# Clears of the modulation's sums and of the late gate's row on GpSimd, and three low halves ahead of a wait

## The chip, the core and the metric

The kernel runs on one core of a Trainium2 chip. The core has five engines that share a memory of 128 partitions: TensorE (matmuls), VectorE, ScalarE, GpSimd, and SyncE, which only issues transfers. Each engine runs its own list of instructions in order and waits on semaphores. Transfers are issued from a queue of SyncE's and one of ScalarE's, and move on the same 16 DMA engines. The metric is the device time of one execution in microseconds. In the rows, PE is TensorE, PEld its weight load, DVE VectorE, ACT ScalarE, POOL GpSimd and SP SyncE; ACTq and SPq are what those engines issue.

## The reference

A model of two blocks of two layers each, over 256 tokens of width 1024, all in fp32. The change is in the first block, where each of the four sublayers (mixer, MLP, mixer, MLP) is modulated by a vector c:

```python
def ada_modulation(c, w, b):
    m = jax.nn.silu(c) @ w + b
    shift, scale, gate = jnp.split(m[:, None, :], 3, axis=-1)
    return shift, scale, 1.0 + gate

for layer in range(DEPTH):
    shift, scale, gate = ada_modulation(c, ada_w[layer, 0], ada_b[layer, 0])
    y = mixer(x * (1.0 + scale) + shift)          # mixer_ab in layer 0, mixer_c in layer 1
    x = layer_norm(DN_ALPHA * x + gate * y, ln_g[layer, 0], ln_b[layer, 0])
    shift, scale, gate = ada_modulation(c, ada_w[layer, 1], ada_b[layer, 1])
    h = x * (1.0 + scale) + shift
    y = jnp.square(jax.nn.relu(h @ w1)) @ w2      # D_FF = 4096
    x = layer_norm(DN_ALPHA * x + gate * y, ln_g[layer, 1], ln_b[layer, 1])
```

The second block (a recurrent mixer, an attention mixer and two MLPs) has no modulation.

## The kernel before

**Weights.** All weights pass as 193 units of 128 x 2048 fp32 (1 MB) through four slots. SyncE loads a unit into `raw`, ScalarE writes its high half (`hi`, line 1279), VectorE the low half `raw - hi` (`low`, line 1859), and TensorE multiplies with both. SyncE loads unit u + 4 when the low half of u is done, so the low halves set when weights are fetched. An fp32 product is made of three products of halves.

**An MLP** (`mlp`, once for each engine) has 16 pairs of units: an up unit (T) gives 256 columns of h @ w1, ScalarE takes them from PSUM (line 1372), VectorE squares them and splits the result into `u_hi` and `u_lo` (lines 1888 to 1902), and a down unit (D) adds u @ w2 into four PSUM banks. TensorE's order is up 0, up 1, down 0, up 2, down 1, up 3, down 2 and so on. VectorE's order at the start is square 0, an affine (the layer norm's gain and bias, lines 1824 and 1825), square 1, an affine, three low halves (for down 1, up 3 and down 2), and then the loop, which begins with square 2.

**Modulations beside it.** Only the first two of the four modulations are made on TensorE. The others are sums on VectorE: `ada_acc` (3 x 1024) is cleared, the bias row `ada_b[s]` is loaded into its first partition, and for each of 8 slices of `ada_w` a multiply with a column of silu(c) is added (lines 1869 and 1945); TensorE then sums the partitions. The call `mlp(0, M0, 2, 1)` makes modulation 2 in MLP 0 (`s_ada` = 2, three parts a slice), and also the gate of modulation 1 (`s_gate` = 1), the late gate: its row `gate_r` is cleared, a bias row is loaded, and 8 slices are added (`late`, line 1882), the first two ahead of the loop. In `mlp(1, M1, None, 3)` there is only the late gate. The mixer of layer 1 makes modulation 3 (two parts); its step `("gate", 2)` stands ahead of it, where the gate of modulation 2 is read out of `ada_acc`.

**Order of the loads.** They are issued by ScalarE in its own order of work. In an MLP, after the high halves of the first units: the layer norm's rows (`load_rows`, lines 1421 and 1422), then `ada_begin` (it waits for the clear by `acc_zero`, then the bias row, line 1357, and three slices, line 1360), then the late gate (it waits for its clear by `late_zero`, bias row, line 1385, and two slices, line 1352).

**Clears.** VectorE makes all four of `ada_acc` and `gate_r` (lines 2021 and 1909): at the start of each MLP for `gate_r`, in MLP 0 after its two affines for `ada_acc`, and at the step `("gate", 2)` for modulation 3. GpSimd does little: small powers for the norms (line 1751), in the order of the same list `STEPS`.

Of the kernel before, what the change touches and what calls it, by code (L numbers as in the profile page):

```python
# [11 lines left out]
KT = D // P  # L12
# [67 lines left out]
def two_block_kernel(nc, stream, ada_w, ada_b, x, x_t, pos, cols, ln_g, ln_b, sinks, g_norm, final_norm,  # L80
# [6 lines left out]
    with ctx:  # L87
# [45 lines left out]
        def arena(at, *shape):  # L133
            n = 1
            for s in shape:
                n *= s
            v = A[:, at:at + n]
            if len(shape) == 2:
                v = v.rearrange("p (a b) -> p a b", a=shape[0])
            return v  # L140
# [7 lines left out]
        ada_acc, gate_r = arena(ADAC, 3 * D), arena(GATE, D)  # L148
# [19 lines left out]
        def adas_before(s_, k=0, part=0):  # L168

            return KT * (0, 2, 4, 7)[s_] + SUMS[s_] * k + part  # L170
# [59 lines left out]
        late_used, late_bias, late_zero = map(sem, ("late_used", "late_bias", "late_zero"))  # L230
# [265 lines left out]
        def _(sp):  # L496
# [33 lines left out]
            def swap(r):  # L530

                tmp, _, to, w = rope_to[r]
                sp.wait_ge(turn_f, r + 1)
                for at in range(0, P, 32):
                    sp.dma_start(A[at:at + 32, to:to + w], A[at ^ 32:(at ^ 32) + 32, tmp + 512 * (r % 2):][:, 0:w]).then_inc(
                        halves_of(r)[0], 16)
# [33 lines left out]
        def _(pe):  # L570
# [300 lines left out]
            def qk_pair(k):  # L871

                heads = [head(k), head(k + 1)]
                at = 4 if k % 4 == 0 else 2
                for h in heads:
                    all_of(h["units"])
                if at == 2:
                    for b in (2, 3):
                        claim(b)
                        held[b] = (exp_done, k + b - 1)  # L880
                elif k >= 4:
                    pe.wait_ge(exp_done, k - 2)
                part = lambda e, t: B[at + e][:, 0:128] if t == 0 else B[at + e][:, 128:384]
                for e in range(2):
                    for t in range(TT):
                        q, kk, _, _ = heads[e]["qk"][0]
                        pe.matmul(part(e, t), q[:, P * t:P * t + P], kk[:, 0:P * (t + 1)], start=t == 0, stop=False,  # L887
                                  skip_group_check=True)
                for t in range(TT):
                    for e in range(2):  # L890
                        q, kk, off, w = heads[e]["qk"][1]
                        pe.matmul(part(e, t), q[off:off + w, P * t:P * t + P], kk[off:off + w, 0:P * (t + 1)], start=False,
                                  stop=False, skip_group_check=True)
                for e in range(2):
                    pe.matmul(B[at + e].rearrange("p (a b) -> p a b", b=256)[:, :, 0:P], ident_b[:, :],
                              causal_b[:, :].unsqueeze(1).to_broadcast([P, 2, P]), start=False, stop=True,
                              skip_group_check=True).then_inc(s_done, 1)
# [153 lines left out]
            for step in STEPS:  # L1051
# [128 lines left out]
                elif kind in ("down", "last"):  # L1180
# [19 lines left out]
                    else:  # L1200
# [3 lines left out]
                                  among_last if n["turned"] == "lb" else None)  # L1204
                elif kind == "bound":
                    b, what, _, _, second, units = a
                    if b in RAW:
                        continue
# [532 lines left out]
        @block.gpsimd  # L1741
        def _(g):
            made = [0]
            g.memset(minus_half[:, :], -0.5).then_inc(half_set, 1)
            g.wait_ge(half_set, 1)

            def root(c0, w, done):

                made[0] += 1
                g.wait_ge(var_ready, made[0])  # L1750
                g.tensor_tensor(rstd[:, c0:c0 + w], ve[:, c0:c0 + w], minus_half[:, 0:w], ALU.pow).then_inc(done, 1)

            for step in STEPS:
                kind, a = step[0], step[1:]
                if kind == "norm2":
                    if a[1] == ML:
                        root(2, 2, root_out)
                    root(0, 2, root_out)
                elif kind == "hg_out":
                    root(8 * a[0], 8, root_out)  # L1760
                elif kind == "bound":
                    b, what = a[0], a[1]
                    if b in RAW:
                        continue
                    for t in range(TT):
                        if b < 4:
                            root(t, 1, root_out)
                        else:
                            root(t, 1, rstd_ready)
                    if what == "lnrms":  # L1770
                        root(2, 2, root_out)
# [3 lines left out]
        def _(v):  # L1775
# [80 lines left out]
            def low(u, s):  # L1856

                v.wait_ge(hi_done, u + 1)
                v.tensor_tensor(w_lo[:, s, :], raw[:, s, :], w_hi[:, s, :], ALU.subtract).then_inc(lo_done, 1)  # L1859
# [12 lines left out]
            def mlp(m, u0, s_ada, s_gate):  # L1872
                p0 = n["plain"]

                def late(k, used, i=0):

                    at = k if isinstance(i, int) else 0
                    col = silu_c[:, k:k + 1] if isinstance(i, int) else silu_c[:, bass.ds(i + k, 1)]
                    loads = 16 * (7 * m + 1) if at == 0 else 16 * (m + 1)
                    v.wait_ge(ld_late[at], loads if isinstance(i, int) else 16 * i + (loads + 16))  # L1880
                    v.wait_ge(late_used, used)
                    v.scalar_tensor_tensor(out=gate_r, in0=late_w[at], scalar=col, in1=gate_r,
                                           op0=ALU.mult, op1=ALU.add).then_inc(late_used, 1)
# [20 lines left out]
                def low_ahead(u, i=0):  # L1904

                    low(4 * i + (u + SLOTS), u % SLOTS)

                if s_gate:
                    v.memset(gate_r, 0.0).then_inc(late_zero, 1)
                for k in range(2):  # L1910
                    square(k, k, n["step"], None)
                    n["step"] += 1
# [1 line left out]
                        normalised()  # L1914
                        affine(k)
                st = n["step"] - 4
                if s_ada:
                    zero_acc()
                    v.wait_ge(ld_bias, 16 * (s_ada + 1))
                for u in range(u0, u0 + 3):  # L1920
                    low_ahead(u)
                if s_gate:
                    v.wait_ge(late_bias, 16 * (m + 1))
                    for k in range(2):
                        late(k, KT * m + k)
# [91 lines left out]
                            f[:, c], e[:, c], lb_c[:, 1, m:m + 1], lb_c[:, 0, m:m + 1], ALU.mult, ALU.add))  # L2017
                    v.tensor_scalar(k, f, -1.0, 1.0, ALU.mult, ALU.add).then_inc(silu_done, 1)

            def zero_acc():  # L2020
                v.memset(ada_acc, 0.0).then_inc(acc_zero, 1)


            v.memset(zero8[:, :], 0.0)
            v.memset(ones[:, :], 1.0).then_inc(consts_ready, 1)
# [45 lines left out]
            for step in STEPS:  # L2071
                kind, a = step[0], step[1:]
# [16 lines left out]
                    angles()  # L2089
                elif kind == "rest":  # L2090
                    low(a[0], a[0] % SLOTS)
                elif kind in ("gate", "gate0"):
                    if kind == "gate":
                        v.wait_ge(gate_ps, a[0] + 1)
                        zero_acc()
                elif kind == "fill":
                    u, part, parts, form, src, reader, dst = a
                    n["plain"] += reader in ("plain", "value")
# [121 lines left out]
                elif kind == "duo":  # L2220
                    g, first, last = a
# [34 lines left out]
                elif kind == "bound":  # L2256
# [227 lines left out]
                    for u in (last_unit + SLOTS - 1, last_unit + SLOTS):  # L2484
                        low(u, u % SLOTS)
                elif kind == "mlp":
                    mlp(a[0], a[1], a[2], a[3])
                elif kind == "hg_start":
                    v.wait_ge(ld_level, 16)
# [54 lines left out]
                elif kind == "hg_out":  # L2544
# [3 lines left out]
                    gate = arena(H_G, TT, D)[:, t, :].rearrange("p (h v) -> p h v", h=HG_HEADS)  # L2548
# [117 lines left out]
```

## Time and profile before

| | |
|---|---|
| median of 3 runs | 1414.03 us (1412.78 to 1414.73) |
| the profiled execution | 1415.55 us, of which the span is 1413.7 |
| TensorE, VectorE, ScalarE, GpSimd busy | 1324.4, 1009.4, 594.2, 13.1 us |
| granted clock of TensorE, mean | 0.975 |
| transfers | 264.18 MB, mean 187 GB/s |

The span is from the first to the last instruction of the profiled execution; times in the rows count from its start. In a timeline a row is: start, duration from the first to the last of the row's instructions, engine, line, operation, tiles, count, and in brackets the idle time before it with what ended it. A granted clock of 1.00 is 2.4 GHz, 0.50 is 1.2 GHz.

### The profile page before, as it was taken

To read this page: it belongs to the slowest core of one execution; us is meant where nothing else is said; L and a number is where in the kernel's file an instruction comes from. 1 tells how busy PE (TensorE), PEld (TensorE's weight loads), DVE (VectorE), ACT (ScalarE), POOL (GpSimd) and SP (SyncE) were. 2 spreads that over 40 slices of the span, in tenths; PEclk is the share of its full clock that TensorE was granted. 3 is DMA by queue.
4 is the path that set the end of the run, shared out by engine and by line. 5 is a ranking of instruction groups with operands and counts; after the bars stand their busy time and mean duration, and the time that the engine had idled before them with its cause. 6 is when DMAs were issued, how large, how long until landed. Compare 5 with 4: busy or idle time off the path is not lost.

```text
span 1413.7 us, 20736 instructions
## 1 busy us (share of the span) xinstructions
PE 1324.4 (94%) x7932; PEld 1119.8 (79%) x7932; DVE 1009.4 (71%) x1358; ACT 594.2 (42%) x803; POOL 13.1 (1%) x22
## 2 busy tenths in 40 slices
PE   5897989999998989999999989999999998999997
PEld 1763677888797868888889987888888877888886
DVE  1768498888888878867687884766668665666665
ACT  2534443433344544343354322534337553533432
POOL 0000000000000000000000000000000000000000
PEclk7899999999999999999999999999999999999999
DMA  9656329878367536665535330555553331455540
GB/s 382 261 194 220 119 90 360 312 262 304 128 244 260 161 120 238 243 226 199 200 129 208 129 120 9 206 202 190 196 178 134 110 145 35 171 219 189 203 150 30
DMA packets 45791, 264.18 MB, mean 187 GB/s; under 512 B 5399, under 2 KB 7063, under 8 KB 19994
## 3 DMA queue, kind: packets, MB, share of 16 engines
q1 hardware_dynamic: 32624, 218.19, 42.2%
q10 hardware_dynamic: 13102, 45.09, 9.2%
q8 instruction: 46, 0.75, 0.2%
q14 instruction: 19, 0.16, 0.0%
HBM read 260.89 MB, written 1.05 MB: 185 GB/s over the span
## 4 chain that ended last, share of the span: by engine, by line
PE 79%; DVE 12%; ACT 3%; DMA 3%; issue 2%; SPq 0%; POOL 0%; ACTq 0%; DVEq 0%; POOLq 0%
PE banks L587 16%; PE banks L589 15%; PE banks L588 15%; PE banks L937 14%; PE banks L940 7%; DMA A<-ada_w 3%; DVE w_lo L1859 2%; PE banks L1237 2%; PE banks L817 1%; PE banks L764 1%; PE banks L799 1%; PE banks L887 1%; ACT w_hi L1279 1%; PE banks L1105 1%; DVE mx L1970 1%
## 5 line engine op out<-in xcount | busy, mean ns | idle before, releaser
L1859 DVE TENSOR_TENSOR w_lo<-raw,w_hi 128x2048 fp32r<-128x2048 f32 x193 | 439.5, 2286 | 118.7 <-ACT w_hi L1279 116.1
L1279 ACT ACTIVATE w_hi<-raw 128x2048 fp32r<-128x2048 f32 x193 | 368.4, 1914 | 226.6 <-PE banks L589 205.1
L937 PE MATMUL banks<-hT,w_hi 128*128 128x512 f32 x896 | 280.8, 395 | 0.0
L587 PE MATMUL banks<-w_hi,R 128*128 128x512 f32 (+1 forms) x624 | 245.7, 394 | 7.1 <-DVE R L1839 3.7
L589 PE MATMUL banks<-w_hi,R 128*128 128x512 f32 (+1 forms) x624 | 242.7, 389 | 0.0
L588 PE MATMUL banks<-w_lo,R 128*128 128x512 f32 (+1 forms) x624 | 242.6, 389 | 0.0
L940 PEld LDWEIGHTS banks<-hT,w_lo 128*128 128x128 f32 x896 | 168.3, 188 | 39.2
L940 PE MATMUL banks<-hT,w_lo 128*128 128x256 f32 x896 | 176.0, 278 | 0.0
L587 PE MATMUL banks<-hT,w_hi 128*128 128x256 f32 x536 | 158.3, 295 | 7.5 <-DVE hT L2329 5.6
L588 PE MATMUL banks<-hT,w_hi 128*128 128x256 f32 x536 | 153.6, 286 | 0.0
L589 PE MATMUL banks<-hT,w_lo 128*128 128x256 f32 x536 | 153.4, 286 | 0.0
L937 PEld LDWEIGHTS banks<-hT,w_hi 128*128 128x128 f32 x896 | 140.6, 189 | 4.4
L587 PEld LDWEIGHTS banks<-w_hi,R 128*128 128x128 f32 x624 | 118.0, 189 | 30.8 <-issue 7.3
L589 PEld LDWEIGHTS banks<-w_hi,R 128*128 128x128 f32 x624 | 117.9, 189 | 24.6
L588 PEld LDWEIGHTS banks<-w_lo,R 128*128 128x128 f32 x624 | 118.1, 189 | 22.0 <-issue 0.7
L1372 ACT ACTIVATE A<-banks 128x512 f32<-128x512 f32 x56 | 33.5, 598 | 216.8 <-PE banks L940 204.1
L587 PEld LDWEIGHTS banks<-hT,w_hi 128*128 128x128 f32 x536 | 104.9, 196 | 12.3 <-ACT A L1295 4.6
L587 PE MATMUL banks<-w_hi,hT 128*128 128x256 f32 (+1 forms) x320 | 103.2, 322 | 10.6 <-DVE hT L1839 8.7
L588 PEld LDWEIGHTS banks<-hT,w_hi 128*128 128x128 f32 x536 | 104.9, 196 | 1.6 <-issue 1.4
L589 PEld LDWEIGHTS banks<-hT,w_lo 128*128 128x128 f32 x536 | 104.7, 195 | 0.0
L589 PE MATMUL banks<-w_hi,hT 128*128 128x256 f32 (+1 forms) x320 | 101.0, 316 | 0.0
L588 PE MATMUL banks<-w_lo,hT 128*128 128x256 f32 (+1 forms) x320 | 100.9, 315 | 0.0
(266 smaller groups left out, 1495.3 us busy)
## 6 DMA issues: line engine op xcount, KB each, us to landing
raw<-stream SPq DMA_DIRECT2D x193, 1024.0 KB, 4.9
A<-ada_w ACTq DMA_DIRECT2D x73, 512.0 KB, 5.6
A<-ada_w SPq DMA_DIRECT2D x5, 1024.0 KB, 17.0
raw<-ada_w SPq DMA_DIRECT2D x3, 1024.0 KB, 7.5
X<-ada_w SPq DMA_DIRECT2D x2, 1024.0 KB, 4.9
A<-ln_g ACTq DMA_DIRECT2D x4, 512.0 KB, 3.6
A<-ln_b ACTq DMA_DIRECT2D x4, 512.0 KB, 5.6
A<-ada_w SPq DMA_DIRECT2D x1, 1536.0 KB
```

The costliest lines, as they stand in the source:

```text
L587: pe.matmul(o, lh, rh, start=start, stop=False, skip_group_check=True)
L588: pe.matmul(o, lh, rl, start=False, stop=False, skip_group_check=True)
L589: return pe.matmul(o, ll, rh, start=False, stop=stop, skip_group_check=True)
L764: m = pe.transpose(B[b][:, P * i:P * i + P], tile, ident[:, :])
L799: pe.matmul(B[d["bank"] + e][:, P * t:P * t + P * (t + 1)], d["q"][r, P * t:P * t + P], d["k"][r, 0:P * (t + 1)], start=t == 0, stop=False ...
L817: m = pe.matmul(B[6 + e][:, P * i:P * i + P], d["p"][e][:, P * i:P * i + P], d["diag"][e][:, 0:P] if i == 0 else d["diag"][e][:, P:2 * P], ...
L937: pe.matmul(two(B[2 * kp + a]), wh[:, kt, P * a:P * a + P], hT[:, :, kt, :], start=kt == 0, stop=False, skip_group_check=True)
L940: last = pe.matmul(B[2 * kp + a][:, 0:256], wl[:, kt, P * a:P * a + P], hT_hi[:, kt, :], start=False, stop=kt == KT - 1, skip_group_check= ...
L1237: m = pe.matmul(bank[:, P * (i % 4):P * (i % 4) + P], tile_at(H_K, h)[:, P * t:P * t + P], tile_at(H_Q, h)[:, P * tq:P * tq + P], start=Tr ...
L1279: act.activation(w_hi[:, s, :], raw[:, s, :], ACT.Copy).then_inc(hi_done, 1)
L1372: act.activation(two(u_f[:, kp, :]), banks[:, 2 * kp:2 * kp + 2, 256:512], ACT.Copy).then_inc(fill_read, 1)
L1859: v.tensor_tensor(w_lo[:, s, :], raw[:, s, :], w_hi[:, s, :], ALU.subtract).then_inc(lo_done, 1)
```

## The change

GpSimd takes the four clears, each behind a wait of its own. It clears `ada_acc` for modulation 2 at the step `row_out`, when TensorE has used the last slice of modulation 1 (`row_w` and the row before it lie in the same place); for modulation 3 at the step `gate`, when the gate has been summed into PSUM (`gate_ps`); and `gate_r` at the step `mlp`, when the residual of the mixer ahead has read the gate (`y_read`). The semaphores `acc_zero` and `late_zero` that ScalarE waits for stay. In an MLP with sums, VectorE's three low halves stand in front of its wait for the bias row (`ld_bias`) instead of behind it.

```diff
--- before.py
+++ after.py
@@ gpsimd, in the loop over STEPS
+                elif kind == "row_out":
+                    g.wait_ge(ada_used, adas_before(1, KT))
+                    g.memset(ada_acc, 0.0).then_inc(acc_zero, 1)
+                elif kind == "gate":
+                    g.wait_ge(gate_ps, a[0] + 1)
+                    g.memset(ada_acc, 0.0).then_inc(acc_zero, 1)
+                elif kind == "mlp" and a[3]:
+                    m = a[0]
+                    g.wait_ge(y_read, 4 * (2 * m + 1))
+                    g.memset(gate_r, 0.0).then_inc(late_zero, 1)
@@ vector, mlp
-                if s_gate:
-                    v.memset(gate_r, 0.0).then_inc(late_zero, 1)
                 for k in range(2):
                     square(k, k, n["step"], None)
...
-                if s_ada:
-                    zero_acc()
-                    v.wait_ge(ld_bias, 16 * (s_ada + 1))
                 for u in range(u0, u0 + 3):
                     low_ahead(u)
+                if s_ada:
+                    v.wait_ge(ld_bias, 16 * (s_ada + 1))
                 if s_gate:
                     v.wait_ge(late_bias, 16 * (m + 1))
@@ vector
-            def zero_acc():
-                v.memset(ada_acc, 0.0).then_inc(acc_zero, 1)
...
-                elif kind in ("gate", "gate0"):
-                    if kind == "gate":
-                        v.wait_ge(gate_ps, a[0] + 1)
-                        zero_acc()
```

## Rows read from the trace of the kernel before

**Rows 1.** The page's part 4, the chain that ended last, by engine.
```profile
PE 79%; DVE 12%; ACT 3%; DMA 3%; issue 2%; SPq 0%; POOL 0%; ACTq 0%; DVEq 0%; POOLq 0%
```

**Rows 2.** Timeline of VectorE at the start of MLP 0 (start us, us, ...).
```profile
200.91 0.91 DVE L1909 MEMSET A<- 128x1024 f32 x1 [0.16 <-issue]
...
210.96 2.62 DVE L2021 MEMSET A<- 128x3072 f32 x1 [0.71 <-DVE X L1825]
215.96 6.69 DVE L1859 TENSOR_TENSOR w_lo<-raw,w_hi 128x2048 fp32r<-128x2048 f32 x3 [2.38 <-DMA A<-ada_b]
...
224.66 1.28 DVE L1882 SCALAR_TENSOR_TENSOR A<-A,silu_c 128x1024 f32<-128x1024 f32 x1 [0.82 <-DMA A<-ada_w]
```

**Rows 3.** Timeline of TensorE in MLP 0: starts of its second and third down stages.
```profile
218.38 0.49 PE L587 MATMUL banks<-w_hi,R 128*128 128x512 f32 x1 [2.16 <-DVE w_lo L1859]
...
231.11 0.40 PE L587 MATMUL banks<-w_hi,R 128*128 128x512 f32 x1
```

**Rows 4.** One stretch of the windows: us, busy times, PEclk, DMA share, GB/s.
```profile
219.00:220.00 1.00, 1.00 (x4) 0.81 (x3) 1.00 (x1) 0.16 (x1) 0.00 (x0) 0.50 1.00 410
```

**Rows 5.** Timeline of ScalarE's queue in MLP 0.
```profile
211.14 0.46 ACTq L1422 DMA_DIRECT2D A<-ln_b  x1
213.61 0.25 ACTq L1357 DMA_DIRECT2D A<-ada_b  x1
...
215.58 0.91 ACTq L1352 DMA_DIRECT2D A<-ada_w  x2
```

**Rows 6.** Timelines of VectorE, ScalarE's queue and TensorE in MLP 1.
```profile
549.93 6.70 DVE L1859 TENSOR_TENSOR w_lo<-raw,w_hi 128x2048 fp32r<-128x2048 f32 x3
...
562.63 1.28 DVE L1882 SCALAR_TENSOR_TENSOR A<-A,silu_c 128x1024 f32<-128x1024 f32 x1 [2.40 <-DMA A<-ada_w]
...
565.82 0.69 DVE L1902 TENSOR_TENSOR R<-A,R 128x512 fp32r<-128x512 f32 x1
...
550.84 0.46 ACTq L1422 DMA_DIRECT2D A<-ln_b  x1
...
566.77 0.40 PE L587 MATMUL banks<-w_hi,R 128*128 128x512 f32 x1
```

**Rows 7.** Timelines of VectorE, ScalarE, its queue and TensorE in layer 1's mixer.
```profile
401.84 2.62 DVE L2021 MEMSET A<- 128x3072 f32 x1 [0.59 <-issue]
...
399.72 1.26 ACT L1434 ACTIVATE A<-banks,ones 128x512 f32<-128x512 f32 x2 [7.37 <-PE banks L1046]
...
403.63 1.93 ACT L1279 ACTIVATE w_hi<-raw 128x2048 fp32r<-128x2048 f32 x1
404.49 0.26 ACTq L1357 DMA_DIRECT2D A<-ada_b  x1
...
437.60 1.65 PE L799 MATMUL banks<-A 64*128 64x128 f32 x8 [4.33 <-DVE A L2147]
```

**Rows 8.** DMA queues (packets, MB, share): 210.8-216, 210.8-226, then 558-560 twice; q10 ScalarE's.
```profile
q10 hardware_dynamic: 334, 1.24, 71.0%
...
q10 hardware_dynamic: 1012, 3.69, 64.7%
...
q1 hardware_dynamic: 75, 0.57, 67.7%
q10 hardware_dynamic: 75, 0.28, 34.5%
```

**Rows 9.** Timelines: the last slice's matmuls, VectorE behind them, a power on GpSimd.
```profile
149.28 1.06 PE L1005 MATMUL banks<-A,silu_c 128*32 128x512 f32 x8
...
151.76 0.48 DVE L1987 TENSOR_SCALAR A<-ident,ri 128x128 f32<-128x128 f32 x2
...
187.71 0.55 DVE L2308 TENSOR_SCALAR A<-X,mv,rstd 128x512 f32<-128x512 f32 x1
...
859.16 1.74 POOL L1751 TENSOR_TENSOR rstd<-ve,minus_half 128x8 f32<-128x8 f32 x1 [4.99 <-DVE ve L2554]
...
860.05 0.42 DVE L1838 CAST R<-A 128x512 fp32r<-128x512 f32 x1
```

## The prediction

> **What bounds the kernel now.** I read the page first: its chain of work is 79% TensorE, 12% VectorE and 3% DMA [rows 1]. So VectorE work that goes away is worth only the TensorE stalls that it causes, and I looked for stalls beside the four clears that the change takes from VectorE.
>
> MLP 0 (the timelines of 196 to 235 us, then the windows): VectorE, when its second affine is done, clears the sums at 210.96 for 2.62, then idles 2.38 for the bias row and begins its three low halves only at 215.96 [rows 2]. TensorE's first down matmul that needs the first of them starts at 218.38 after 2.16 of idling [rows 3], and after that stall its granted clock is 0.50, the lower level of 1.2 GHz [rows 4]. ScalarE's queue explains the wait: the layer norm's rows go out at 211.14, and the bias row only at 213.61, when the clear has ended; the two late gate slices go out from 215.58 [rows 5].
>
> MLP 1 is the useful neighbour. It has the same layer norm rows and late gate, but no sums, so there the three lows already follow the affine with nothing between. The queue's second row load goes out at 550.84 against 211.14: MLP 1 is MLP 0 shifted by 339.70. Its third down stage starts at 566.77 with no stall; its u is complete at 565.82 + 0.69 = 566.51, so it had 0.26 us to spare, and what ran last before it was the second late gate slice, whose multiply had waited until 562.63 for its data [rows 6].
>
> The mixer of layer 1: VectorE clears from 401.84 for 2.62, ScalarE's bias load goes at 404.49, and TensorE later idles 4.33 for the roped keys, on a chain of ada_w loads begun there [rows 7]. The four clears of the two MLPs and the mixer are all that is in question; elsewhere the kernel stays as it is.
>
> **Part 1, what goes from VectorE.** Two clears of 2.62, two of 0.91 and one wait of 2.38 [rows 2, 7]. The late row's 0.91 in MLP 0 stands ahead of the first square, but the second square waits for ScalarE all the same, so I count 0 to 0.9 and take nothing; in MLP 1 TensorE does not stall, and it is worth 0.
>
> **Part 2, MLP 0 up to the first down stage.** The bias load no longer waits for a clear. ScalarE's queue goes on after its second row load (211.14 and its 0.46), so everything behind it goes out some 2.0 earlier: bias at 211.6, three ada_w slices to 213.2, the late bias and the two late slices by 214.4. VectorE starts the lows at 549.93 - 339.70 = 210.2, 5.7 earlier. The stall of 2.16 goes. Undisturbed, TensorE would start its third down stage at 566.77 - 339.70 = 227.07; it started at 231.11 [rows 3, 6], so stall and low clock together cost 4.04, of which the clock is about 1.7 (4.04 less the stall, which measured from the modelled end before it may be 2.3). If nothing is late next, this part gives -4.0.
>
> **What is late next.** The lows free their raw slots, so SyncE's three 1 MB weight loads also go out 5.9 earlier, at about 212.5, 214.7 and 217.0, as in MLP 1. In the kernel before, they went out behind the ada_w and late slices: from 210.8 to 216 ScalarE's queue alone moved bytes (1.24 MB), and its 3.69 MB were through by 226 [rows 8]. Now they compete, with 3.69 - 1.24 = 2.45 MB still to come on ScalarE's queue at 216, and the late slices are the last of it. In MLP 1, where they do compete, SyncE's queue moved 0.57 MB and ScalarE's 0.28 in the same 2 us: twice as much, 0.425 MB/us together [rows 8]. MLP 1 has only 0.26 to spare with 1.5 MB fewer in that queue, so MLP 0 must now wait. When does the second late slice land?
> - Upper bound: all of both queues must pass first, 2.45 + 3.15 = 5.60 MB, 13.2 us, 229.2. At 2 to 1 it comes out there too, since the weights are through first.
> - Equal shares: 2 x 2.45 / 0.425 = 11.5 us, 227.5.
> - Lower bound, strictly in order of issue with one weight load ahead: 3.50 / 0.425 = 8.2 us, 224.2.
>
> I take 228.5, near the 2 to 1 of the row. From the late multiply to a complete u is 566.51 - 562.63 = 3.88 [rows 6]. So the third down stage starts at 232.4 in place of 231.11: +1.3. TensorE has then idled 5.3 from 227.07, and the low clock after it costs 1.7 as it did after 2.16: MLP 0 is **+3.0** and not -4.0. Bounds: 224.2 gives 228.1 and -3.0 (with a full clock cost -1.3); 229.2 and half a microsecond to land gives +4.2. Behind that stage VectorE is in time again (low, three sums of 1.28 like the late multiply's, low, square: its next u about 2 us ahead of need), so the shift is passed on unchanged.
>
> **Part 3, the mixer.** GpSimd can start its clear when the gate rows are in PSUM, the moment at which ScalarE reads them (399.72), and at VectorE's 2.62 it ends at 402.3. ScalarE comes to its bias load when its second high half has started, 403.63, instead of 404.49. So the ada_w chain, up to the stall at 437.60, begins 0.8 earlier [rows 7]: **-0.8**. If GpSimd needs twice VectorE's time the clear ends at 405.0 and this becomes +0.5; if every load still lands when it did, 0.
>
> **Part 4, the clears on GpSimd.** No row shows a long clear on GpSimd. Three of the four have much room: the sums' first from about 150.3 (the last ada_w slice's matmuls, 149.28 and 1.06) to 211.6, the late rows 25 us. What they can cost is VectorE's own time beside them. From below: a GpSimd power of 1.74 us at 859.16 ran while VectorE's cast at 860.05 took 0.42, its usual time, so 0 [rows 9]. From above: the diagonal multiplies at 151.76 would wait for the clear's end at 150.34 + 2.62 = 152.96, 1.2, on the chain there; the centred half at 187.71 for a clear of 0.91 begun at about 187.3, 0.5 [rows 2, 9]: 1.7 together. The power touched only 8 columns, so the row is weak evidence; I take **+0.4**.
> The Trainium skill ("SBUF — State Buffer", "Who interferes with whom") says that casts and scalar multiplies of VectorE which stream through two ports share them with GpSimd under an exclusive lock, and the loser waits for the whole instruction; two-input operations don't mind a GpSimd that only writes. The cast at 860.05 does not show it; by the rule the sum would have the upper 1.7 here.
>
> **Sum.** +3.0 - 0.8 + 0.4 = +2.6 us. The profiled execution took 1415.55, with a span of 1413.7 and 1.85 around it, and is 1.5 above the median of the runs, 1414.03; the shift holds for both, so I put 1414.03 + 2.6 = **1416.6**. A difference under 0.2% (2.8 us) is about what a measurement of this kernel can't tell from none.
>
> **Rivals.**
> - *Nothing is late next* (the other side): the late slices land before 223.2 and MLP 0 gives its 4.0, the mixer 0.8: 1409.2. For it: the second landed by 224.66 before [rows 2], issued 2 us later. Against: then the weight loads were behind them. It decides at a landing of 223.2 (227.07 - 3.88). Chance 0.10.
> - *The queues share in the late slices' favour*: landing between 224.2 and 226.5, start of the stage 228.1 to 230.4, low clock 0 to 1.7; with the mixer and the clears -3.4 to +0.6: 1410.6 to 1414.6. For it: the slices are issued first, and in MLP 1 the two shares were measured with no ada_w slices queued. Against: 2 to 1 is what MLP 1 shows. Chance 0.20.
> - *A clear on GpSimd holds up VectorE* at 151.76 and 187.71 for its whole length: 1.3 more than in the sum, +3.9: 1417.9. Decided by a cast or scalar multiply that starts within a clear. Chance 0.20. The rule of the Trainium skill ("SBUF — State Buffer", "Who interferes with whom") would make it so.
> - *The change doesn't free ScalarE*: a GpSimd clear slower than 3.9 us (403.63 - 399.72) holds the mixer's bias load; at 8 us (three times VectorE's) it goes out at 407.7, 3.2 later than before, which is 4.0 more than in the sum: 1420.6. Chance 0.08.
> - *The forecast*, weight loads first and little on VectorE: +1.3 to +3.7, 1415.3 to 1417.7. Chance 0.42.
>
> Faster by over 0.2%: the first rival and half of the second's lower part, 0.18. Slower: about 0.4 of the forecast's 0.42 (0.17), the third rival (0.19) and the fourth (0.07), 0.43. Within 0.2%: the rest, 0.39. The range of 8 in 10, 1411.2 to 1419.2, leaves out the first rival, the edge of the second and the fourth; the forecast's own is 1415.3 to 1417.7.
>
> **What would show it.** In MLP 0: low halves right behind the affine (about 210.2), no stall at the first of the loop's down stages, the late multiplies waiting some 10 us for ada_w, and a TensorE stall of about 5 us some 11 us after the old one, named after the u, with a granted clock of 0.5 behind it. In the mixer: the bias load 0.8 earlier against the gate rows. At the diagonal multiplies after the last ada_w slice: no gap, or one as long as the clear. It would be wrong if the late multiplies started within 13 us of the affine's end, or if the mixer's stall were shorter by much more than 0.8.

## Result and the profile after

The changed kernel takes 1423.62 us (median of 10 runs), the kernel before 1415.36 in the same session (10 runs): a ratio of 1.0055, 95% interval 1.0038 to 1.0071, which is 7.8 us slower (5.4 to 10.0). The forecast was 1416.6, that is +2.6, with a range up to 1419.2: the sign of its sum is right, its size is not. (1.3 of the distance is the kernel before itself, whose first three runs had a median of 1414.03.) The profiled execution of the changed kernel took 1427.3 with a span of 1425.4; it is 3.7 above the median of its ten runs, so I compare it stage by stage and not by its end. The ratios of the experiments leave out four executions of 2196 to 4804 us (one each of e4 and e5, two of the kernel before), which the medians still count.

The chain of work that ended last now has DMA in it at 4%, which had 3% [rows 1]:

```profile
PE 80%; DVE 10%; DMA 4%; ACT 3%; issue 2%; SPq 0%; ACTq 0%; POOL 0%; DVEq 0%; POOLq 0%
```

**MLP 0.** The timeline of VectorE, against [rows 2]; the three low halves now begin where the affine (from 213.99 for 1.22) ends:

```profile
215.25 6.69 DVE L1869 TENSOR_TENSOR w_lo<-raw,w_hi 128x2048 fp32r<-128x2048 f32 x3
234.71 2.69 DVE L1892 SCALAR_TENSOR_TENSOR A<-A,silu_c 128x1024 f32<-128x1024 f32 x2 [12.77 <-DMA A<-ada_w]
239.31 0.69 DVE L1912 TENSOR_TENSOR R<-A,R 128x512 fp32r<-128x512 f32 x1
```

TensorE, against [rows 3], and the windows, against [rows 4]. The stall of 2.16 at the second down stage is gone; in its place stands one of 7.81 at the third, and the clock behind it is the lower level again (0.50, the third figure from the end of a row of the windows):

```profile
240.05 0.80 PE L587 MATMUL banks<-w_hi,R 128*128 128x512 f32 x1 [7.81 <-DVE R L1912]
248.40 0.61 PE L937 MATMUL banks<-hT,w_hi 128*128 128x512 f32 x2
```
```profile
241.00:242.00 1.00, 1.00 (x4) 0.73 (x3) 1.00 (x1) 0.00 (x0) 0.00 (x0) 0.50 0.06 16
244.00:245.00 1.00, 1.00 (x4) 0.74 (x3) 1.00 (x2) 0.00 (x0) 0.00 (x0) 0.50 0.90 352
```

ScalarE's queue, against [rows 5], the weight loads on SyncE's, and the queues' bytes (packets, MB, share) in three stretches of 2 us, 219 to 221, 225 to 227 and 233 to 235:

```profile
215.79 0.34 ACTq L1421 DMA_DIRECT2D A<-ln_g  x1
216.65 0.30 ACTq L1357 DMA_DIRECT2D A<-ada_b  x1
218.93 1.01 ACTq L1352 DMA_DIRECT2D A<-ada_w  x2
```
```profile
217.71 4.74 SPq L498 DMA_DIRECT2D raw<-stream  x3
```
```profile
q10 hardware_dynamic: 134, 0.51, 62.7%
...
q1 hardware_dynamic: 84, 0.56, 66.1%
q10 hardware_dynamic: 82, 0.29, 35.1%
...
q10 hardware_dynamic: 154, 0.53, 65.6%
q1 hardware_dynamic: 23, 0.07, 8.4%
```

The row 225 to 227 is the 2 to 1 that [rows 8] showed in MLP 1, now with ada_w slices queued. It holds until the weights are through at 233; then ScalarE's queue is alone again, and the late slices are the last of it.

**The diagonal multiplies and the centred half**, against [rows 9]: GpSimd's clears in its timeline, then VectorE's multiplies in its own. The first pair took 0.48 before and ends here at 155.86, the clear at 155.72; the half took 0.55:

```profile
153.06 2.66 POOL L1763 MEMSET A<- 128x3072 f32 x1 [107.31 <-PE banks L1005]
190.84 0.94 POOL L1770 MEMSET A<- 128x1024 f32 x1
413.20 2.66 POOL L1766 MEMSET A<- 128x3072 f32 x1 [14.94 <-PE banks L1046]
```
```profile
154.36 1.50 DVE L1994 TENSOR_SCALAR A<-ident,ri 128x128 f32<-128x128 f32 x2
...
191.32 0.75 DVE L2308 TENSOR_SCALAR A<-X,mv,rstd 128x512 f32<-128x512 f32 x1
```

**The mixer of layer 1**, against [rows 7]: ScalarE and its queue, then TensorE at the scores. The third clear ends at 415.86, and the bias row goes out at once, while the first high half is still running and 1.19 before the second:

```profile
413.18 1.27 ACT L1434 ACTIVATE A<-banks,ones 128x512 f32<-128x512 f32 x2 [7.29 <-PE banks L1046]
...
414.81 1.92 ACT L1279 ACTIVATE w_hi<-raw 128x2048 fp32r<-128x2048 f32 x1
415.90 0.26 ACTq L1357 DMA_DIRECT2D A<-ada_b  x1
...
417.09 1.93 ACT L1279 ACTIVATE w_hi<-raw 128x2048 fp32r<-128x2048 f32 x1
```
```profile
448.47 0.93 PE L799 MATMUL banks<-A 64*128 64x128 f32 x8 [2.73 <-DVE A L2147]
```

**Stages.** To compare executions I use differences of starts. "MLP 0" is from the issue of its first layer norm row (215.79 above, 210.78 before) to GpSimd's power in the next norm:

```profile
386.73 0.54 POOL L1751 TENSOR_TENSOR rstd<-ve,minus_half 128x1 f32<-128x1 f32 x1 [194.95 <-DVE ve L1809]
```
In the kernel before, with the start of the up stage that follows its third down stage, which is needed below:
```profile
210.78 0.34 ACTq L1421 DMA_DIRECT2D A<-ln_g  x1
...
236.56 0.62 PE L937 MATMUL banks<-hT,w_hi 128*128 128x512 f32 x2
...
374.90 0.54 POOL L1751 TENSOR_TENSOR rstd<-ve,minus_half 128x1 f32<-128x1 f32 x1 [187.63 <-DVE ve L1799]
```

386.73 - 215.79 = 170.94 against 374.90 - 210.78 = 164.12. "Diagonals" is from one low half to the next around the diagonal multiplies (before: 149.37 and 167.15). "Mixer" is from ScalarE's reading of the gate rows to the power of the mixer's own norm (before: 399.72 and 519.01). The kernels e1 to e12 are those of the next section.

| execution | MLP 0 | diagonals | mixer |
|---|---|---|---|
| before / once more (e10) | 164.12 / 163.81 | 17.78 / 17.78 | 119.29 / 118.71 |
| after / once more (e11) | 170.94 / 170.71 | 18.79 / 18.82 | 115.24 / 115.39 |
| e1 clears alone | 164.49 | 18.79 | 115.71 |
| e2 order alone | 168.55 | 17.78 | 117.16 |
| e3 late slices first | 160.08 | 21.29 | 114.23 |
| e4 quiet clears | 170.50 | 17.79 | 115.70 |
| e5 mixer's clear alone | 163.79 | 17.81 | 115.91 |
| e6 late first and quiet | 160.08 | 17.83 | 115.74 |
| e7 weight loads split | 168.18 | 18.80 | 117.27 |
| e8 clear in pieces | 170.21 | 18.08 | 114.25 |
| e9 bias row ahead | 170.65 | 18.82 | 115.23 |
| e12 late first, VectorE's clears | 160.08 | 17.78 | 118.80 |

The 21.29 of e3 has a low clock in it (0.83 over 150 to 165, where the kernel before has 1.00).

Between the second of these low halves (167.15 before, 170.76 after) and the first layer norm row lies a stretch that the table leaves out. It takes 43.63 and 43.60 in the two executions of the kernel before and 45.03 and 44.80 in those of the changed kernel. The centred half stands in it, and a stretch of low clock behind it, which ends later in the changed kernel; the windows, 29 us behind the low half in each, after and then before:

```profile
200.00:201.00 1.00, 1.00 (x6) 1.00 (x6) 1.00 (x2) 0.00 (x0) 0.00 (x0) 0.50 0.00 0
...
196.00:198.00 2.00, 2.00 (x19) 2.00 (x18) 2.00 (x2) 0.00 (x0) 0.00 (x0) 1.00 0.45 61
```

MLP 1, which the prediction put at 0, shows no gain: from the last power ahead of it to the next it takes 185.96 and 186.83 before, 186.86 and 186.88 after.

### The profile page after: what moved, and what is told of

The parts are those of the page before. It is cut to its first block, busy times and chain, and to the rows that moved or that the text cites. A ratio compares the mean times of both kernels' runs of the same rounds, so it can differ in the third digit from the quotient of the medians.

```text
span 1425.4 us, 20737 instructions
## 1 busy us (share of the span) xinstructions
PE 1331.4 (93%) x7932; PEld 1125.5 (79%) x7932; DVE 1004.3 (70%) x1354; ACT 594.4 (42%) x803; POOL 20.2 (1%) x26
## 4 chain that ended last, share of the span: by engine, by line
PE 80%; DVE 10%; DMA 4%; ACT 3%; issue 2%; SPq 0%; ACTq 0%; POOL 0%; DVEq 0%; POOLq 0%
PE banks L587 16%; PE banks L588 16%; PE banks L589 16%; PE banks L937 14%; PE banks L940 7%; DMA A<-ada_w 4%; PE banks L1237 2%; DVE w_lo L1869 2%; PE banks L817 1%; PE banks L764 1%; PE banks L799 1%; PE banks L887 1%; PE banks L1105 1%; ACT w_hi L1279 1%; PE banks L832 1%
```

## Experiments

**e1 and e2: one half of the change each.** e1 keeps the clears on GpSimd and restores the order; e2 has only the order.

```diff
 e1, against after                            e2, against before
+    if s_ada: v.wait_ge(ld_bias, ...)        +    for u in range(u0, u0 + 3): low_ahead(u)
     for u in range(u0, u0 + 3): low_ahead(u)      if s_ada: v.wait_ge(ld_bias, ...)
-    if s_ada: v.wait_ge(ld_bias, ...)        -    for u in range(u0, u0 + 3): low_ahead(u)
```

> The changed kernel with VectorE's wait for the bias row back in front of the three low halves of MLP 0; the clears stay on GpSimd. Theory (the early lows send SyncE's weight loads out among the late gate slices, and these get a third of the bytes): the lows begin some 3.7 us later than in the changed kernel, the weight loads go out as much later, the late multiply starts some 14.5 to 16 us behind the affine's end instead of 19.5, and TensorE's stall before the third down stage falls from 7.8 to about 3 to 4: 3 to 5 us faster than the changed kernel. Rival (the clears on GpSimd, or ScalarE's queue being two microseconds early, are what costs): late multiply, stall and time as in the changed kernel.

> The kernel before with only the order changed: the three low halves in front of the wait for the bias row in MLP 0; every clear stays on VectorE. Theory (weight loads against late slices): lows begin at about 3 us behind the affine's end (the clear is still there), no stall at the first of the loop's down stages, late multiply some 17 us behind the affine's end, TensorE idles 3 to 5 us before the third down stage with the low clock behind it: MLP 0 is 1 to 4 us longer than in the kernel before; the mixer of layer 1 and the diagonal multiplies (0.48 us) as before: 1416 to 1419 us. Rival (the order itself is harmless and the clears make the loss): MLP 0 is 2 to 4 us shorter than before, 1411 to 1413.

e1: 1416.54, ratio to before 1.0012 (0.9993 to 1.0031). e2: 1421.74, ratio 1.0039 (1.0018 to 1.0059). So the order makes the loss in MLP 0: with it alone the stage is 4.4 longer, without it 0.4. The rest of the changed kernel's 6.8 needs both parts: in e2 the lows still begin 3.25 behind the affine's end, after VectorE's clear, and in the changed kernel right behind it. VectorE, TensorE and the queues (221 to 223, then 225 to 227) of e1:

```profile
218.59 6.70 DVE L1869 TENSOR_TENSOR w_lo<-raw,w_hi 128x2048 fp32r<-128x2048 f32 x3 [6.12 <-DMA A<-ada_b]
225.21 2.68 DVE L1892 SCALAR_TENSOR_TENSOR A<-A,silu_c 128x1024 f32<-128x1024 f32 x2
```
```profile
221.02 0.49 PE L587 MATMUL banks<-w_hi,R 128*128 128x512 f32 x1 [2.52 <-DVE w_lo L1869]
```
```profile
q10 hardware_dynamic: 229, 0.84, 102.1%
...
q1 hardware_dynamic: 108, 0.81, 97.3%
q10 hardware_dynamic: 4, 0.01, 1.1%
```

Here ScalarE's queue moves alone until 223, when little of its work is left, and the weights come after it. The late multiplies run straight behind the lows, with no wait at all: the expected stall of 3 to 4 us before the third down stage isn't there, and MLP 0 is 6.4 shorter than in the changed kernel's first profile, where 3 to 5 was expected. What I had not expected is the wait of 6.12: without a clear to wait for, the bias row was issued 0.86 behind the first layer norm row (2.83 in the kernel before), and the lows began 5.54 behind it (5.18 before). Nothing was gained by freeing the queue.

In e2 (TensorE):

```profile
235.49 0.80 PE L587 MATMUL banks<-w_hi,R 128*128 128x512 f32 x1 [6.03 <-DVE R L1902]
```

The stall was expected at 3 to 5, and the time at 1416 to 1419: both came out above.

**e9: the bias row ahead of the layer norm rows.** To see what e1's wait is.

```diff
 scalar, mlp (against e1)
+    if s_ada: ada_bias(s_ada)       # the row's load, out of ada_begin
     if m < 2: load_rows(m, 1)
     if s_ada: ada_begin(s_ada)      # now the three slices alone
```

> The clears alone on GpSimd, with the three lows behind the wait for the bias row as in the kernel before, but ScalarE issues that bias row ahead of the two layer norm rows. Theory (freeing ScalarE's queue gained nothing for the bias row because it lands behind the two 512 KB layer norm rows in front of it): the row lands about 2.5 us after its issue instead of 4.7, the lows begin 2 to 3.5 us earlier than with the clears alone (some 3 us behind the affine's end instead of 6.1), the weight loads follow, and the late multiply comes that much nearer to the changed kernel's 19.5 us behind the affine's end: a stall of 1 to 4 us before the third down stage. Rival (the row's own single partition is what takes 4.7 us): lows as with the clears alone.

One run, 1428.0 us. ScalarE's queue, VectorE and TensorE:

```profile
216.23 0.25 ACTq L1356 DMA_DIRECT2D A<-ada_b  x1
216.52 0.34 ACTq L1427 DMA_DIRECT2D A<-ln_g  x1
```
```profile
218.09 6.70 DVE L1875 TENSOR_TENSOR w_lo<-raw,w_hi 128x2048 fp32r<-128x2048 f32 x3 [2.44 <-DMA A<-ada_b]
...
236.55 1.28 DVE L1898 SCALAR_TENSOR_TENSOR A<-A,silu_c 128x1024 f32<-128x1024 f32 x1 [1.76 <-DMA A<-ada_w]
```
```profile
240.49 0.80 PE L587 MATMUL banks<-w_hi,R 128*128 128x512 f32 x1 [7.81 <-DVE R L1918]
```

The row is there 1.9 us after its issue (218.09 - 216.23), where it took 4.7 in e1: it had stood behind two transfers of 512 KB. And the lows, 2.4 behind the affine's end, give the whole stall of the changed kernel and not a part: by this one execution it isn't the lows' start in proportion that counts, but whether the weight loads come in while the slices still have bytes to move.

**e3, e6 and e12: the late slices first.** In e3 ScalarE issues the late bias and slices ahead of the modulation's, and VectorE waits in that order; e6 adds e4's waits (below); e12 is the same order in the kernel before with the lows ahead, all clears on VectorE.

```diff
 scalar, mlp                                   vector, mlp
-    if s_ada: ada_begin(s_ada)               -    if s_ada: v.wait_ge(ld_bias, ...)
     if s_gate: late bias, two late slices         if s_gate: wait for late_bias, late(0), late(1)
+    if s_ada: ada_begin(s_ada)               +    if s_ada: v.wait_ge(ld_bias, ...)
```

> The changed kernel, but in MLP 0 ScalarE issues the late bias and the two late gate slices ahead of the modulation's bias row and ada_w slices, and VectorE's wait for that bias row stands behind the late multiplies. Theory (the late slices are late only because they are last in a queue that gets a third of the bytes): the late multiply starts some 12.5 us behind the affine's end as in MLP 1, TensorE does not idle before the third down stage, and MLP 0 is 9 to 11 us shorter than in the changed kernel and about 4 shorter than before: 1412 to 1415 us. Rival (ScalarE's queue as a whole is late): the three ada_w slices become what TensorE waits for one stage on, and the time falls by less than 4 us.

> The changed kernel with the late gate slices issued ahead of the modulation's and with GpSimd's first clear behind the diagonal multiplies and its row clear behind the first lows of the loop. If the three findings add up: MLP 0 some 160 us from its layer norm rows to the next norm (164.1 before, 170.9 changed), diagonal multiplies 0.48, mixer 114 to 117: 5 to 8 us faster than the kernel before, 1408 to 1411. If the lock costs nothing end to end: no faster than the run with the late slices first alone (1413.6).

> The kernel before with every clear still on VectorE; the three lows stand in front of the wait for the bias row, and ScalarE issues the late slices ahead of the modulation's. Theory (in MLP 0 the order of the loads decides, and where the clears run is worth little): no stall before the third down stage, MLP 0 some 161 us from its layer norm rows, 2 to 4 us faster than the kernel before: 1412 to 1414. Rival (the clear on VectorE still delays the lows or the late slices' row enough): MLP 0 above 163 us, no faster than the kernel before.

e3: 1413.57, ratio to before 0.9978 (0.9957 to 0.9999). e6: 1411.32, 0.9967 (0.9949 to 0.9986). e12: 1414.36, 0.9978 (0.9958 to 0.9999). All three have 160.08 in MLP 0 and no stall of TensorE at its start: 10.9 less than the changed kernel and 4.04 less than before (3.73 against its second execution), as the prediction worked out for nothing being late. VectorE in e3, where the second late multiply stands 11.5 behind the affine's end (218.28):

```profile
226.25 1.28 DVE L1892 SCALAR_TENSOR_TENSOR A<-A,silu_c 128x1024 f32<-128x1024 f32 x1 [1.24 <-issue]
229.79 1.28 DVE L1892 SCALAR_TENSOR_TENSOR A<-A,silu_c 128x1024 f32<-128x1024 f32 x1 [2.26 <-DMA A<-ada_w]
```

The modulation's slices, last now, cost TensorE nothing. By e12 the stage needs none of GpSimd's clears for this. e6 has the lowest median of all kernels here, 4.7 below before where 5 to 8 was expected; e3, e6 and e12 are not told apart by their intervals.

**e7: SyncE's weight loads in halves.**

```diff
 sync, load (against after); ScalarE's wait counts 32 a unit
-    sp.dma_start(raw[:, s, :], w).then_inc(raw_full[s], 16)
+    sp.dma_start(raw[:, s, 0:1024], w[:, 0:1024]).then_inc(raw_full[s], 16)
+    sp.dma_start(raw[:, s, 1024:2048], w[:, 1024:2048]).then_inc(raw_full[s], 16)
```

> The changed kernel, but SyncE loads each 1 MB weight tile as two transfers of 1024 columns, so that a row of a weight transfer is 4 KB as in the ada_w slices, and no longer 8 KB. Theory (the engines take the queues' rows in turn, so bytes go 2 to 1 because the rows are 2 to 1): while both queues have work in MLP 0 each moves about half, and the late multiply starts some 1 to 2.5 us earlier behind the affine's end than 19.5 us. Rival (the ratio goes by the queue or by what was there first): 2 to 1 stays and the late multiply is where it was. The time may also move by what twice as many transfers cost elsewhere.

1426.86, ratio to before 1.0078 (1.0049 to 1.0107): no faster than the changed kernel in all, though MLP 0 is 2.7 shorter. Its queues at 224 to 226, VectorE and TensorE:

```profile
q10 hardware_dynamic: 115, 0.42, 51.5%
q1 hardware_dynamic: 117, 0.42, 51.1%
```
```profile
229.76 1.28 DVE L1894 SCALAR_TENSOR_TENSOR A<-A,silu_c 128x1024 f32<-128x1024 f32 x1 [9.84 <-DMA A<-ada_w]
232.14 1.28 DVE L1894 SCALAR_TENSOR_TENSOR A<-A,silu_c 128x1024 f32<-128x1024 f32 x1 [1.10 <-DMA A<-ada_w]
```
```profile
236.09 0.80 PE L589 MATMUL banks<-w_hi,R 128*128 128x512 f32 x1 [5.87 <-DVE R L1914]
```

With rows of 4 KB in both queues each moves 0.42 MB in 2 us, and the second late multiply begins 18.9 behind the affine's end instead of 20.8 (the first, of which the expectation spoke, 16.6 instead of 19.5). The packets were near one to one in the changed kernel too (84 and 82): the queues share by packets, and 2 to 1 in bytes was 8 KB against 4.

**e4 and e8: GpSimd's first clear.** e4 lets it wait for the eight diagonal multiplies, and the clear of `gate_r` for the first lows of the loop; e8 makes it in six pieces.

```diff
 gpsimd (against after), e4                    e8
+    g.wait_ge(duo_ready, 8)                   -    g.memset(ada_acc, 0.0)...
     g.memset(ada_acc, 0.0)...                 +    for c in range(0, 3 * D, 512):
...                                            +        p = g.memset(ada_acc[:, c:c + 512], 0.0)
+    g.wait_ge(lo_done, a[1] + 2)              +    p.then_inc(acc_zero, 1)
     g.memset(gate_r, 0.0)...
```

> The changed kernel, but GpSimd's first clear of the sums waits until VectorE's eight diagonal multiplies are through, and its clear of the late gate's row until the first lows of the loop are done. Theory (a clear on GpSimd holds up a scalar multiply of VectorE for its whole length): the diagonal multiply falls from 1.50 to 0.48 us, the centred half from 0.75 to 0.55, and the time by about 1.2 us. Rival (the long multiply of the one profile was something else): they keep their lengths or the time does not move by more than 0.5 us.

> The changed kernel, but GpSimd's first clear of the sums is made of six clears of 512 columns, some 0.5 us each. Theory (VectorE's scalar multiply waits for the GpSimd instruction that holds the port, and for that one alone): the diagonal multiply that took 1.50 us takes at most 1.0 (0.48 and what is left of one piece). Rival (the loser waits until GpSimd has nothing more to do): it takes 1.5 us or more, as the six pieces end no earlier than the one clear.

e4: 1419.59, ratio to before 1.0032 (1.0013 to 1.0052); the multiplies take 0.48 and the half 0.55 again, and the stretch of the diagonals is 17.79, 1.0 less than after. The 1.2 us by themselves are below what the times can tell: e4's interval overlaps that of the changed kernel. e8, one run, 1423.81; GpSimd and VectorE:

```profile
153.14 2.99 POOL L1764 MEMSET A<- 128x512 f32 x6 [107.31 <-PE banks L1005]
```
```profile
154.44 0.76 DVE L1996 TENSOR_SCALAR A<-ident,ri 128x128 f32<-128x128 f32 x2
```

The multiplies ended at 155.20 with the pieces running until 156.13: VectorE waits for the piece that is under way and not for GpSimd to be done.

**e5: the mixer's clear alone.** The kernel before with only the third clear on GpSimd.

```diff
 gpsimd                                        vector
+    elif kind == "gate":                     -    elif kind in ("gate", "gate0"):
+        g.wait_ge(gate_ps, a[0] + 1)         -        if kind == "gate":
+        g.memset(ada_acc, 0.0)...            -            v.wait_ge(...); zero_acc()
```

> The kernel before with one part of the change: GpSimd does the clear in front of the mixer of layer 1; the other three clears and the order stay. Theory (ScalarE's queue issues ahead of its activations, so the bias load goes out at the clear's end and not behind the second high half): the bias load 2.7 us after the gate rows are read instead of 4.8, the stall at the scores shorter or gone, the mixer from the gate rows to the next norm about 115.5 us instead of 119.3, the run 2 to 4 us faster than before. Rival (the profile of the kernel before had an unlucky mixer, and the clear itself is worth the 0.8 us of the prediction or nothing): 118 us or more here, less than 1 us faster.

1415.14 against 1416.26, ratio 1.0001 (0.9982 to 1.0020): no gain that can be measured, which speaks for the rival. The stage itself did as the theory expected, and not the rival's 118 or more: the bias load 2.72 behind the gate rows (405.89 and 403.17), the stall at the scores 1.87, the mixer 115.91.

**e10 and e11: both kernels profiled once more**, unchanged.

> The kernel before, profiled once more, to see which stages differ between two executions of one kernel. If the longer stretch in front of the gate rows (12.5 us between the two halves' norms where the profile of the kernel before had 9.3) is chance, it can show here too; MLP 0 from its layer norm rows on should repeat 164.1 within 0.7 us, and the stretch from the last low half at the diagonal multiplies to the next should repeat 17.8.

> The changed kernel, profiled once more: MLP 0 from its layer norm rows 170.9 within 0.7 us, a diagonal multiply of 1.5 us, TensorE's stall before the third down stage 7.5 to 8 us; the stretches that no part of the change touches may differ by 1 to 3 us.

1420.92 and 1424.87, one run each. MLP 0 and the diagonals repeat within 0.31, TensorE's stall is 7.60. Between the two powers of the norm ahead of the mixer the kernel before took 9.25 in its first profile and 12.47 in this one; the changed kernel 10.88 and 10.84. Nothing of the change stands there, so such 1 to 3 us of a single execution say nothing.

## Why the prediction went wrong

**What the stages add up to.** MLP 0 +6.9 (means of the two executions of each), the diagonals +1.0, the stretch between them +1.3, the mixer -3.0 (mean of ten executions with GpSimd's clear, 115.5, of four with VectorE's, 118.5): +6.2, within the measured 5.4 to 10.0. The step that failed is "What is late next": it had MLP 0 at +3.0, because it let the late slices land too early and the low clock cost too little. The clears in Part 4 were too cheap as well, and the mixer in Part 3 hid a part of both, if its -3.0 holds.

**MLP 0: the mechanism was right, two terms were too small.** Undisturbed, the stage gains 4.04: shown by e3, e6 and e12. The weight loads go 2 to 1 ahead of the late slices: shown by the queues' rows, by e2 (the order alone makes the stall), and by e1 and e3, each of which takes one of its conditions away. The predicted third down stage was 232.4 - 210.78 = 21.6 behind the first layer norm row, the measured one 240.05 - 215.79 = 24.3, so TensorE idled 7.8 and not 5.3. I had put the landing of the second late slice at 228.5, though my own sum for 2 to 1 came to 229.2, the upper bound: the 0.7 had no reason. Moved to the times of the kernel before, the second multiply began at 231.0 (the pair starts at 234.71 and its second 1.35 later, at 236.06; 215.79 - 210.78 = 5.01 is the shift). The queues' bytes end at about 235, which is 230 there, and the two slices came so close together that the second multiply also stood behind the first. So even the bound was short: it let the bytes run at 0.425 MB/us to the end, but the last stretch moved 0.60 MB in 2 us, and it gave the first multiply no time.

**The low clock** was taken at 1.7, as after a stall of 2.16. From the start of the third down stage to the next up stage is 236.56 - 231.11 = 5.45 in the kernel before, at full clock, and 248.40 - 240.05 = 8.35 here: 2.9. After 6.03 of idling (e2) it is 7.72, so 2.3. But the length of the stall alone doesn't set the cost. In e4 the stage after 7.75 of idling takes 245.24 - 237.28 = 7.96, so 2.5, and in e8 after 7.73 it takes 7.68, so 2.2; e4:

```profile
237.28 0.80 PE L587 MATMUL banks<-w_hi,R 128*128 128x512 f32 x1 [7.75 <-DVE R L1914]
245.24 0.61 PE L937 MATMUL banks<-hT,w_hi 128*128 128x512 f32 x2
```

In the changed kernel 2.6 of a later start and 1.2 of the clock are the 3.8 between +3.0 and the measured +6.8.

**The share in the late slices' favour**, the second rival, is refuted by the rows: packets go one to one, so 4 KB rows lose to 8 KB rows, and being issued first didn't help once the weight loads were there too.

**Freeing the bias row.** The prediction listed the wait of 2.38 as saved. It was not the clear alone that it came from: with the clears gone (e1) the lows start no earlier, since the row lands behind two layer norm rows; e9 shows it by its landing in 1.9. Against the first layer norm row the lows gained 2.5 by the order (5.18 behind it before, 2.67 in e2) and 3.2 more by VectorE's clear going (0.54 ahead of it in the changed kernel).

**The clears on GpSimd.** I took +0.4 from a row that I called weak, between 0 and 1.7. It is at least +1.2: 1.0 at the diagonals (17.78 to 18.79, back to 17.79 in e4) and 0.2 at the half. That is the third rival, and the rule of the Trainium skill ("SBUF — State Buffer", "Who interferes with whom") agrees, in both directions: the scalar multiplies wait for the instruction under way (e8), and the two-input low half at 151.97, beside the clear from 153.06, takes its usual 2.28. The whole stretch with the half in it grew by 1.3, and is back at 43.63 in e4; but e2, with no clear on GpSimd, has 45.06 there, so that the clears make the other 1.1 isn't shown. The power of 8 columns beside a cast was no example of a long clear. The fourth rival is out: GpSimd clears 3072 columns in 2.66 where VectorE took 2.62.

**The mixer: the step is wrong, its worth is open.** I had ScalarE come to the bias load with its second high half, 0.8 earlier than before. It went out at the clear's end, 2.72 behind the gate rows instead of 4.77, while the first high half still ran; the second high half, which began 1.19 later, stands in front of that load in ScalarE's list. So its queue issues ahead of the activations. TensorE's stall at the scores fell from 4.33 to 2.73, by 1.6 and not 0.8, which the prediction had named as a sign of being wrong. The profiles give -3.0 for the stage. The timed run of that part alone (e5) gives +0.1 (-2.5 to +2.8), and the stages' sums with -3.0 come out 1 to 2.3 us below the times in the changed kernel, e1, e3, e4 and e6 too; in e2 and e12, which have no such term, the sums are 0.5 above and 0.8 below. So I don't count the 3.0 as shown; with the 0.8 that I had, the changed kernel's parts would sum to +8.4, which the measured interval holds as well. What takes the rest back I couldn't find in the stages behind.

**The range** held bounds of +4.2 for MLP 0 and 1.7 for the clears, but no case with both near their ends: 4.2 - 0.8 + 1.7 = +5.1 is 1419.1, already its top. A low clock that costs more than 1.7, which it held nowhere, goes beyond.

## What to carry to other kernels

When VectorE or any engine frees a buffer earlier, list the transfers that the freeing lets go and what they will share the DMA engines with: here 5.7 us gained on VectorE cost 7 us on TensorE, because three weight loads were let in among slices that were needed first. Put the loads in the order in which they are needed, the first needed first in its queue, before the work is pulled ahead: two exchanged calls in ScalarE's list, with VectorE's waits in the same order, turned a loss of 7.8 us into a gain of 3.1 (e3, 0.1 to 6.1). Before moving a clear to GpSimd, look for scalar multiplies of VectorE beside it: here one pair waited for the clear's end.

## What the hardware showed that I had not expected

- Two queues with work share by packets: 84 to 82 packets were 0.56 to 0.29 MB, and with rows of equal size 0.42 to 0.42.
- A bias row of 12 KB takes 4.7 us behind two broadcast rows of 512 KB in its own queue, and 1.9 ahead of them.
- ScalarE issued a transfer at 415.90 while an activation of 1.92 us was under way, and ahead of one at 417.09 that stands in front of it in its list.
- The low clock behind a stall cost 1.7 us after 2.2 and 2.5 of idling and 2.1 to 2.9 after 5.9 to 7.8; after nearly the same 7.7 to 7.8 it cost 2.2 (e8), 2.5 (e4) and 2.9 (the changed kernel).
